# Two transformer blocks on one core: paired first outputs after each norm, a folded modulation sum, grouped semaphore clears and a zero-padded rotary key

## The reference

```
first_block, for i in 0, 1:
    h = h + 0.5 * swiglu(rmsnorm(h), ffn1)
    u = rmsnorm(h) @ w_in
    y = concat(latent attention, bidirectional mLSTM, Fourier mixer)(u)
    h = h + y @ w_out
    h = h + 0.5 * swiglu(rmsnorm(h), ffn2)
    h = h + sigmoid(rmsnorm(h) @ ple_w_gate) * rmsnorm(p[i] @ ple_w_proj)
x = rmsnorm(h)
second_block, for l in 0, 1:
    mod = silu(c) @ ada_w[l] + ada_b[l]            # 6 x 1024 shifts, scales and gates
    y = concat(window attention, HGRN2, gated delta)((rmsnorm(x) * (1 + sc_m) + sh_m) @ w_in)
    x = x + gt_m * (y @ w_out)
    x = x + gt_f * swiglu(rmsnorm(x) * (1 + sc_f) + sh_f)
```

## Time and profile before

| | |
|---|---|
| median of 3 runs | 3873.01 us (3872.42 to 3882.36) |
| profiled execution | 3878.38 us, span of its instructions 3876.6 us |
| PE busy | 3701.6 us, 95% |
| DVE busy | 2217.1 us, 57% |
| ACT busy | 1297.6 us, 33% |
| POOL busy | 722.8 us, 19% |
| mean granted TensorE clock | 0.962 |
| read from HBM | 340.60 MB, 88 GB/s |

### The profile page before, as it was taken

How to read it: one execution, slowest core, us unless ns; L and a number is a source line. 1 busy time by engine, 2 the same in 40 slices (tenths; PEclk the granted TensorE clock), 3 DMA queues, 4 the chain that set the end, 5 groups by cost and what they waited for, 6 DMA issues and landing times. The chain is left out here.

```text
span 3876.6 us, 42134 instructions
## 1 busy us (share of the span) xinstructions
PE 3701.6 (95%) x16630; PEld 2875.4 (74%) x16630; DVE 2217.1 (57%) x2994; ACT 1297.6 (33%) x1873; POOL 722.8 (19%) x434
## 2 busy tenths in 40 slices
PE   8999998999999999998999989888999999989999
PEld 6888733888878888536888876685888767867887
DVE  6555557655575445457655575665444657755443
ACT  3223235522242223335322343444222343443221
POOL 3432002343213430001433022020000020200000
PEclk9999998999999999998999999798999998989999
DMA  4443200444324342102444222001233220012332
GB/s 170 141 138 106 97 16 30 135 140 133 120 93 136 127 144 87 54 23 91 135 140 136 88 82 60 1 1 66 93 93 103 82 72 21 1 48 82 98 100 82
DMA packets 92947, 345.43 MB, mean 89 GB/s; under 512 B 10832, under 2 KB 11088, under 8 KB 91856
## 3 DMA queue, kind: packets, MB, share of 16 engines
q1 hardware_dynamic: 92752, 342.74, 27.4%
HBM read 340.60 MB, written 2.10 MB: 88 GB/s over the span
## 5 line engine op out<-in xcount | busy, mean ns | idle before, releaser
L383 ACT ACTIVATE w_hi<-raw 128x1024 fp32r<-128x1024 f32 (+2 forms) x540 | 559.6, 1038 | 1903.7 <-PE ps L327 1888.4
L325 PE MATMUL ps<-xs_hi,w_hi 128*128 128x512 f32 x2472 | 982.1, 397 | 34.5 <-DVE xs_lo L544 16.4
L327 PE MATMUL ps<-xs_hi,w_lo 128*128 128x512 f32 x2472 | 970.6, 393 | 0.0
L326 PE MATMUL ps<-xs_lo,w_hi 128*128 128x512 f32 x2472 | 970.4, 393 | 0.0
L393 DVE TENSOR_TENSOR w_lo<-raw,w_hi 128x1024 fp32r<-128x1024 f32 (+2 forms) x540 | 677.6, 1256 | 123.5 <-ACT w_hi L383 122.9
L325 PEld LDWEIGHTS ps<-xs_hi,w_hi 128*128 128x128 f32 x2472 | 469.2, 190 | 160.4 <-issue 33.8
L326 PEld LDWEIGHTS ps<-xs_lo,w_hi 128*128 128x128 f32 x2472 | 469.8, 190 | 99.0 <-issue 3.6
L327 PEld LDWEIGHTS ps<-xs_hi,w_lo 128*128 128x128 f32 x2472 | 469.2, 190 | 98.9
L325 PE MATMUL ps<-hd_hi,w_hi 128*128 128x512 f32 x1320 | 518.8, 393 | 4.8 <-DVE hd_lo L486 3.7
L326 PE MATMUL ps<-hd_lo,w_hi 128*128 128x512 f32 x1320 | 516.0, 391 | 0.0
L327 PE MATMUL ps<-hd_hi,w_lo 128*128 128x512 f32 x1320 | 516.0, 391 | 0.0
(11 more groups left out here) (454 smaller groups left out, 4335.1 us busy)
## 6 DMA issues: line engine op xcount, KB each, us to landing
raw<-in_ffn_gu SPq DMA_DIRECT2D x264, 512.0 KB, 3.9
arena<-in_ada SPq DMA_DIRECT2D x64, 768.0 KB, 5.7
raw<-in_ffn_dn SPq DMA_DIRECT2D x96, 448.0 KB, 3.4
raw<-in_in_t SPq DMA_DIRECT2D x60, 512.0 KB, 3.7
raw<-in_ffn_dn SPq DMA_DIRECT2D x48, 512.0 KB, 3.5
raw<-in_out SPq DMA_DIRECT2D x32, 512.0 KB, 3.7
raw<-in_pleg SPq DMA_DIRECT2D x16, 512.0 KB, 3.6
raw<-in_in_r SPq DMA_DIRECT2D x8, 512.0 KB, 3.8
```

What stands on the lines that cost most here:

```text
L325: T.matmul(bank, lhs_hi(k), rhs_hi(k), start=(first and k == 0), stop=False)
L326: T.matmul(bank, lhs_hi(k), rhs_lo(k), start=False, stop=False)
L327: mm = T.matmul(bank, lhs_lo(k), rhs_hi(k), start=False, stop=(last and k == kt - 1))
L383: A.activation(self.hi[:, n % HL, 0:size], raw[:, n % RAW, 0:size], ACT.Copy).then_inc(self.high_done, 1)
```

## The change

1. `paired_products` does the first two outputs after each norm together: for each input tile, three products for one and three for the other. It is used in `FeedForward` (gate and up of the first hidden tile), `GateEmbed` and `Project`. The product for R comes after both. `GateEmbed` uses four banks instead of two.
2. `ShiftEmit` sums seven tiles' squares with one product and adds the last tile's square with a second; VectorE's addition of the last one comes after the tiles are made. `idle_products` puts FP32 products of constants with an unused result between and after these (1, or 3 in `FinalShift`, between; 3 after), and 8 at the end of the mLSTM stage.
3. In the last step of `GateEmbed`, the weight's high and low part come after the sigmoid and, where a `ShiftEmit` follows, after a Sqrt of one column.
4. `Adaptive`: VectorE transposes each 128x768 chunk of the sum in blocks of 32x32 and reduces it to 24 columns (`dve_fold`, after hidden tiles 9, 13 and 18 and after down output 5 of the last chunk); TensorE then does 4 products with a tiled 32x32 identity as weights, ahead of output 7. The identity is a new transfer at the start.
5. Semaphores are cleared in ranges of neighbouring numbers; the block ahead of the first `mixer2` is gone. `HeadNorms` objects share semaphores with the one before.
6. Latent attention: the rotary key stands in two tiles with the other 64 rows zero, filled by GpSimd (`kr_half`), and its product takes 128 rows. The values of the third head are multiplied after step 17 instead of 14.

```diff
+    def clear_all(sp, sems):
+        numbers = sorted(sem.num for sem in sems)
+        start = 0
+        for i, number in enumerate(numbers):
+            if i + 1 == len(numbers) or numbers[i + 1] != number + 1:
+                sp.sem_clear(range(numbers[start], number + 1))
+                start = i + 1
...
+    def paired_products(pe, x, n, banks, before):
+        for k in range(DT):
+            for i in range(2):
+                w_hi, w_lo = ring.tile(ring.hi, n + i), ring.tile(ring.lo, n + i)
+                if k == 0:
+                    ring.ready(pe, n + i)
+                if i == 0:
+                    before(k)
+                T.matmul(banks[i], w_hi(k), x.hi[:, k, :], start=(k == 0), stop=False)
+                T.matmul(banks[i], w_hi(k), x.lo[:, k, :], start=False, stop=False)
+                mm = T.matmul(banks[i], w_lo(k), x.hi[:, k, :], start=False, stop=(k == DT - 1))
+                if k == DT - 1:
+                    mm.then_inc(ring.used, 1)
+
+    def idle_products(bank, count):
+        for _ in range(count):
+            T.matmul(bank, C("ident"), cst[:, 0:S], start=True, stop=True)
...
     class ShiftEmit(Emit):
         def dve(self, dve, k):
-            self.add(dve, k)
+            if k < DT - 1:
+                self.add(dve, k)
         def pe(self, pe):
-            self.summed(pe)
-            T.matmul(ps[6][:, :], ones(P), hsq[:, :], start=True, stop=True).then_inc(self.sums, 1)
+            pe.wait_ge(self.added, DT - 1)
+            T.matmul(ps[6][:, :], ones(P), hsq[:, :], start=True, stop=False)
+            idle_products(ps[7][:, :], self.ahead)
+            pe.wait_ge(self.squares, DT)
+            T.matmul(ps[6][:, :], ones(P), sq[:, (DT - 1) % 2, :], start=False, stop=True).then_inc(self.sums, 1)
+            idle_products(ps[7][:, :], 3)
...
     class Adaptive:
         def pe(self, pe):
-            pe.wait_ge(self.added, 2 * NADA)
-            for j in range(24):
-                mm = T.matmul(ps[7][:, j:j + 1], ada_acc[:, j * P:(j + 1) * P], C("one"), start=True, stop=True)
+            pe.wait_ge(self.folded, 2 * AN)
+            for b in range(P // FOLD):
+                mm = T.matmul(ps[7][FOLD * b:FOLD * (b + 1), 0:24], fold, ada_red[:, :, b], start=True, stop=True)
             mm.then_inc(self.summed, 1)
+        def dve_fold(self, dve, c):
+            across = aw[:, 0, :] if c == AN - 1 else tmp.rearrange("p a s -> p (a s)")[:, 0:AC]
+            blocks = AC // FOLD
+            dve.wait_ge(self.added, DT * (c + 1))
+            if c:
+                dve.wait_ge(self.folded, 2 * c)
+            V.transpose(across, ada_acc[:, c * AC:(c + 1) * AC]).then_inc(self.folded, 1)
+            dve.wait_ge(self.folded, 2 * c + 1)
+            V.reduce_sum(ada_acc[:, c * blocks:(c + 1) * blocks], across.rearrange("p (b r) -> p b r", r=FOLD), AX.X) \
+             .then_inc(self.folded, 1)
+            dve.wait_ge(self.folded, 2 * c + 2)
...
     class GateEmbed:
+        BANKS = (0, 1, 4, 5, 4, 5, 4, 5)
         def pe(self, pe):
+            paired_products(pe, self.x, self.n0, (ps[self.BANKS[0]][:, :], ps[self.BANKS[1]][:, :]), self.source.tile_wait(pe))
+            self.norm.pe(pe)
+            pe.wait_ge(self.down_read, len(CHUNKS) * DT)
+            for j in range(2, DT):
...
         def act(self, act):
             for j in range(DT):
-                ring.high(act, self.n0 + j + HL)
+                if j < DT - 1:
+                    ring.high(act, self.n0 + j + HL)
...
                 A.activation(gn[:, j % 2, :], gn[:, j % 2, :], ACT.Sigmoid).then_inc(self.sig, 1)
+                if j == DT - 1:
+                    if isinstance(self.emit, ShiftEmit):
+                        A.activation(junk[:, :], C("one"), ACT.Sqrt)
+                    ring.high(act, self.n0 + j + HL)
...
     def mixer1_attention(l, m, work):
+        Y_AFTER = (6, 10, 17, 18)
+        kr_half = [mx[:, c, 0:S] for c in range(2)]
...
-                        T.matmul(score[m % 3], qr[b:b + 64, hd // 2, q], kr[b:b + 64, :], start=False, stop=True) \
-                         .then_inc(scores_ready, 1)
+                        T.matmul(score[m % 3], qr[:, hd // 2, q], kr_half[hd % 2], start=False, stop=True).then_inc(scores_ready, 1)
...
+            @st.block.gpsimd
+            def _(pool):
+                pool.wait_ge(conv_ready, 2)
+                for c in range(2):
+                    G.memset(kr_half[c][halves_of[1 - c], :], 0.0)
+                pool.wait_ge(rotated, 3)
+                for c in range(2):
+                    G.tensor_copy(kr_half[c][halves_of[c], :], kr[halves_of[c], :]).then_inc(kr_ready, 1)
...
     def mixer1_mlstm(l, m, work, spectrum):
+                idle_products(ps[2][:, :], 8)
...
     for l in range(DEPTH):
-        if l == 0:
-            Stage.clear_last()
```

More of the change, by code:

```diff
@@ L357, in clear @@
         def clear(self, sp):
[L358 to L359 removed]
+            clear_all(sp, self.landed + [self.high_done, self.low_done, self.used])
         def load(self, sp, n):
@@ L553, in __init__ @@
             self.shifted = isinstance(source, ShiftEmit)
-            self.sums, self.rooted, self.inverted = [st.sem(tag + n) for n in ("_sums", "_rooted", "_inverted")]
+            self.inverted = st.sem(tag + "_inverted")
+            if not self.shifted:
+                self.sums, self.rooted = st.sem(tag + "_sums"), st.sem(tag + "_rooted")
         def pe(self, pe, consts=None):
             if consts:
-                pe.wait_ge(consts, 16)
+                pe.wait_ge(consts, 32)
             if not self.shifted:
@@ L766, in __init__ @@
             self.l, self.half = l, half
-            self.landed, self.scaled, self.added, self.used, self.summed = [
-                st.sem(f"a{l}{half}_{n}") for n in ("landed", "scaled", "added", "used", "summed")]
+            self.landed, self.scaled, self.added, self.used, self.folded, self.summed = [
+                st.sem(f"a{l}{half}_{n}") for n in ("landed", "scaled", "added", "used", "folded", "summed")]
         def sp(self, sp, n):
@@ L896, in pe @@
                 for j in range(t0, t0 + nt):
-                    for a in range(2):
+                    if j == 0:
+                        paired_products(pe, self.x, n, (ps[0][:, :], ps[1][:, :]), self.source.tile_wait(pe))
+                        self.norm.pe(pe, self.consts)
+                        n += 2
+                    for a in range(2 if j else 0):
                         ring.ready(pe, n)
@@ L912, in pe @@
                 for o in range(DT):
-                    if self.adaptive and c == len(CHUNKS) - 1 and o == 4:
+                    if self.adaptive and c == len(CHUNKS) - 1 and o == DT - 1:
                         self.adaptive.pe(pe)
@@ L991, in dve @@
                             self.embed.dve_scale(dve, 2 * (j - E_AFTER - 2) + i)
+                    if self.adaptive and j in FOLD_AT:
+                        self.adaptive.dve_fold(dve, FOLD_AT[j])
                     if self.tables and j in (3, 5):
@@ L1004, in dve @@
                         self.emit.dve(dve, o)
+                    if self.adaptive and c == len(CHUNKS) - 1 and o == 5:
+                        self.adaptive.dve_fold(dve, AN - 1)
                     n += 1
@@ L1350, in pe @@
         def pe(self, pe):
-            for j in range(self.count):
+            paired_products(pe, self.x, self.n0, (ps[0][:, :], ps[1][:, :]), self.source.tile_wait(pe))
+            self.norm.pe(pe)
+            for j in range(2, self.count):
                 n = self.n0 + j
@@ L2026, in __init__, with wait_summed, wait_inverted, wait_ready @@
             self.rows = slice(0, 2 * self.n)
-            self.squares, self.summed, self.rooted, self.inverted, self.spread, self.ready = [
-                st.sem(tag + name) for name in ("_squares", "_summed", "_rooted", "_inverted", "_spread", "_ready")]
+            self.norms_before = after.norms_before + 1 if after else 0
+            self.tiles_before = after.tiles_before + after.n if after else 0
+            if after:
+                self.squares, self.summed, self.rooted = after.squares, after.summed, after.rooted
+                self.inverted, self.spread, self.ready = after.inverted, after.spread, after.ready
+            else:
+                self.squares, self.summed, self.rooted, self.inverted, self.spread, self.ready = [
+                    st.sem(tag + name) for name in ("_squares", "_summed", "_rooted", "_inverted", "_spread", "_ready")]
+        def wait_summed(self, eng):
+            eng.wait_ge(self.summed, self.norms_before + 1)
+        def wait_inverted(self, eng, pieces=1):
+            eng.wait_ge(self.inverted, self.norms_before + pieces)
+        def wait_ready(self, eng, tiles):
+            eng.wait_ge(self.ready, self.tiles_before + tiles)
         def act_square(self, act, r):
@@ L2077, in __init__ @@
             self.turned, self.rotated = st.sem("turned"), st.sem("rotated")
```

(10 more changed lines are left out.)

91 lines of the change are left out of this document (43 added, 48 removed).

## The result

The changed kernel takes 3814.09 us (median of 4 runs, 3811.68 to 3815.43) beside 3875.05 us: a ratio of 0.9839, interval 0.9822 to 0.9856, so 61 us less, 56 to 69. I forecast 77 us less; the time lies in the range, and a fifth of the gain is missing.

The account below looks back on a forecast made before the run. TensorE was taken as the bound, busy 3701.6 of 3876.6 us. The terms summed to -77 us from the 3873.0 us median, giving 3796 us; their bounds gave 13 us either side, stretched towards rivals 1 to 3 to a range of 3781 to 3820.

Parts of the forecast that it names:

- adaptive sum: Four feed-forwards' last chunks: the sum costs 34.3 us now and 5.6 after folding on VectorE; -29 us, bounds -25 and -31.
- into the third feed-forwards: Handover, twice: earlier root and paired outputs end the second output at 2714.2 instead of 2719.7; -10.8 us for both.
- into the last projection: Handover at 3067.8: second output ends 6.1 us earlier, less a new 1.1 us wait at the row sums; -5.0 us.
- between the blocks: Handover before the second block, at 2257.1: later last square, and 1.1 us lost at the row sums; 0 (-2 to +2).
- gate into the next layer: Embedding's gate: pair shortens the handover by 5.6 us, output 4's waits in the gate cost +1.2; -4.4 us.
- start: Kernel start: tiles 4 to 7 land late for both outputs, end near 30.6 rather than 33.6, extra transfer 0.4; -2.7 us.
- handovers without shift: Five other handovers: no wait now and none after, though R comes 5.4 us later; +0.3 us.
- clears, block, DFT transfer: Range clears and removed block: 6.3 us at the block, 2.3 at the end, 2.6 for DFT matrices; -11.2 us.
- attention, both layers: Score period falls from 2.5 to 2.2 us, copies cost 1.4, tail gains 2.7; -11.8 us, bounds -4 and -15.
- fillers after mLSTM: Eight fillers at both mLSTM stages' ends keep the next stage's first products off the slow clock; -2.5 us for both.
- Rivals 1 and 2: 1: fillers run at 1.2 GHz and delay, 3813 us, chance 0.12; 2: VectorE sets attention score period, 3808 us, chance 0.12.
- rival 3: Handovers win half of their 23 us because moved weights hold VectorE and ScalarE and tiles come later: 3808 us, chance 0.1.

Follow-up runs that it names:

- The second series: The changed kernel with nothing edited, measured again beside the kernel before in a later series: ratio 0.9830, interval 0.9813 to 0.9848.

## Why the prediction was right, and where it was off

| term | predicted | at the places |
|---|---|---|
| adaptive sum | -29 | -31.0 |
| into the third feed-forwards | -10.8 | -9.8 |
| into the last projection | -5.0 | -2.8 |
| between the blocks | 0 | +2.7 |
| gate into the next layer | -4.4 | -4.6 |
| start | -2.7 | -2.4 |
| handovers without shift | +0.3 | +4.7 |
| clears, block, DFT transfer | -11.2 | -11.8 |
| attention, both layers | -11.8 | -10.4 |
| fillers after mLSTM | -2.5 | -3.3 |
| what is left, most of it lower clock | 0 | +2.0 |
| sum | -77 | -66.7 (span) |

- **The step that failed** is "The other five non-shifted handovers have no wait now and get none". I followed R to its first reader on VectorE and stopped there. In the second feed-forward the late reading pushes VectorE's work on the second hidden tile back, there that work takes 2.8 us longer, the embedding's sum of squares stands behind it on VectorE, ScalarE's third square waits for that sum, the fourth copy stands behind the square, and TensorE needs the copy. That costs 1.8 us twice, plus 0.56 twice at the projections' row sums: 4.7 us for the 0.3 of this term. The kernel with pairs only where tiles are late shows that the pairs were the cause. (Besides the gates, which have their own price, there are four such handovers and not five.)
- **"I again lose 1.1 at the row sums"** was right in size (1.15) and incomplete. In the first profile 8 main products behind each of these waits ran at 0.42 us, 1.5 us more a place. This is most of the miss of both second-block projections. At the last one all traces agree that the wait brings them; at the border they come in four of nine, so there the wait alone doesn't decide.
- **The handover windows** were the strong part: the root 3.1 us after the last product for 2.9, 48 products at 0.227, and ends within 0.6 us. But I gave the pair all the credit, also at the projections, where the runs show it is worth nothing.
- **The adaptive sum** came out 2.0 us better, for one mis-sized term: the small products cost 0.2 us and not 0.9, and the wait 0.5 as forecast. What the sum cost before was right: 34.3 us, against 31.0 gained and 4 x 0.87 still paid, 34.5. The transposes went as the reduction's row said. The section Rules for kernel authors of "VectorE: DVE Perf Modes" in the Trainium skill warns of the reduction; here 128x768 takes 0.95 us, no longer than the transpose's 0.97, and but for the wait of 0.5 us at each last fold its cost is VectorE's alone.
- **The clears** added up at their places, but the block's worth was taken at the border only. Behind it 6.2 of 9.3 us came back in one pair of kernels, and 3.9 of 9.1 in the means of all. (The table has the block by its wait, 6.4 us; from before to after the border itself got 8.4 us shorter and the stage behind it 5.9 us longer, and both rests are in the last row but one.)
- **Attention**: the period (2.16 for 2.2) and the copies were right; a lower clock of 1.5 us at the first attention's start came on top.
- **The time**: of the 16 us between -77 and -61, ten are in the table and six are the choice of profiled executions. The second series gives -66. The measured 3814 us lies 18 above my 3796 and inside the range only because I had stretched its upper end for rivals 1 to 3; the bounds of the terms alone ended at 3809. Rivals 1 and 2 fell. Of rival 3 only the size came: all handovers together won 12.2 us of the 22.6 forecast, but by R's lateness and the lower clock behind it, not by late tiles. That the range held is in part luck.
- **What stays open**: what decides where the groups of 8 slow products fall. They appear and vanish between executions of one kernel, and a group that a filler removes can be followed by a new one 50 us later. Nor is it shown that GpSimd's addition is what makes VectorE's two passes slow.

## What to carry to other kernels

When an input is moved later, follow it through every engine's queue until TensorE, not to its first reader: here what stood behind the first reader cost 4.7 us where I had priced 0.3. Pair outputs only where the trace shows TensorE waiting tile by tile, and look at what the paired weights or the later norm hold up. Work that is a poor fit for TensorE (one-column products of full weights) is cheap on an engine that idles, as long as its last piece ends before the consumer gets there.

## What was not expected of the hardware

- Eight records of products with 32-column weights and 24 columns show as 0.28 us in all, 0.21 to the next start; eight one-column ones with 128-column weights show as 0.95.
- Identical instructions in two executions of one kernel differed by 3.25 us in a stretch of 137 us, with a granted clock of 0.96 and 0.93.
- A pause of some 9 us ahead of a stage of small products was followed by a stage 6.2 us shorter in one pair of kernels; over all profiles the two groups of stages overlap.
- A wait of about 1.1 us in a stretch that was otherwise busy was followed, at the last projection, by a group of some 8 products at 0.42 us in nine profiles of nine; with a filler in it the clock stayed at 1.00.
- VectorE's cast and its subtraction of 128x512 took 1.70 and 2.22 us beside an addition of GpSimd, with medians of 0.43 and 0.69.
